# One quarter of a weight load split at partition 119

## The reference, cut to what matters

```python
for e in range(N_EXPERTS):
    gate = jnp.minimum(hf @ w_gate[e] + b_gate[e], SWIGLU_LIMIT)
    up = jnp.clip(hf @ w_up[e] + b_up[e], -SWIGLU_LIMIT, SWIGLU_LIMIT)
    act = gate * jax.nn.sigmoid(SWIGLU_ALPHA * gate) * (up + 1.0)
    y = y + combine[:, e:e + 1] * (act @ w_down[e] + b_down[e])
```

## Time and profile before

| | us |
|---|---|
| median of 3 runs | 1167.24 (1167.2 to 1167.29) |
| the profiled execution, its own time | 1170.19 |
| its span in the trace | 1168.4 |
| PE busy | 1123.5 (96%) |
| DVE busy | 361.7 (31%) |
| ACT busy | 256.8 (22%) |

### The profile page before, as it was taken

One profiled execution on the slowest core, in us unless ns is written; L12 is line 12 of the kernel. 1 busy time (PEld: TensorE's weight loads), 2 busy tenths in 40 slices (PEclk: granted clock), 3 DMA queues, 4 the chain that ended last, 5 costly groups with the idle time before them and its releaser, 6 DMA issues.

```text
span 1168.4 us, 14913 instructions
## 1 busy us (share of the span) xinstructions
PE 1123.5 (96%) x6081; PEld 560.4 (48%) x6081; DVE 361.7 (31%) x877; ACT 256.8 (22%) x528; POOL 15.6 (1%) x20
## 2 busy tenths in 40 slices
PE   8999999999999999999999989998989998999988
PEld 8998989874343434243433333333333433443333
DVE  5566765641213222212121212121212121222213
ACT  6566554431101101111111110111010111110102
POOL 1000000000000000000000000000000000000000
PEclk9999999989999999999999989999999998999999
DMA  9865546789999999999999999999999999999995
GB/s 301 293 179 182 163 153 223 300 358 416 426 429 426 428 435 431 430 431 431 431 430 432 431 432 431 430 430 430 430 430 434 430 431 429 430 426 430 427 424 216
DMA packets 52782, 445.52 MB, mean 381 GB/s; under 512 B 3715, under 2 KB 32057, under 8 KB 37489
## 3 DMA queue, kind: packets, MB, share of 16 engines
q1 hardware_dynamic: 50666, 439.83, 90.5%
q0 software_dynamic: 1248, 4.20, 1.3%
q10 hardware_dynamic: 806, 0.59, 0.2%
HBM read 443.47 MB, written 1.13 MB: 381 GB/s over the span
## 4 chain that ended last, share of the span: by engine, by line
PE 68%; DMA 27%; ACT 1%; issue 1%; DVE 1%; ACTq 0%; SPq 0%; DVEq 0%
PE psum L1312 25%; DMA ring<-in_w_up 25%; PE psum L1337 13%; PE psum L1235 5%; PE psum L953 4%; PE psum L955 4%; PE psum L954 4%; PE psum L1250 4%; DMA ring<-in_w_down 2%; PE psum L1258 2%; PE psum L1044 1%; PE psum L998 1%; PE psum L1080 1%; PE psum L1056 1%; ACT pieces L708 1%
## 5 line engine op out<-in xcount | busy, mean ns | idle before, releaser
L1312 PE MATMUL psum<-ring,xT 128*64 128x512 f32 x960 | 435.1, 610 | 36.0 <-DMA ring<-in_w_up 35.1
L1313 PE MATMUL psum<-ring,xT 128*64 128x512 f32 x960 | 435.3, 610 | 0.0
L1312 PEld LDWEIGHTS psum<-ring,xT 128*64 128x64 f32 x960 | 132.1, 140 | 313.3 <-issue 298.6
L1337 PE MATMUL psum<-ring,guT 128*64 128x512 f32 x992 | 226.5, 598 | 1.4 <-DMA ring<-in_w_down 0.7
L1750 DVE COPY gu<-psum 128x512 f32<-128x512 f32 x32 | 33.5, 1047 | 574.2 <-PE psum L1313 574.2
L1313 PEld LDWEIGHTS psum<-ring,xT 128*64 128x64 f32 x960 | 132.1, 140 | 0.0
L1337 PEld LDWEIGHTS psum<-ring,guT 128*64 128x64 f32 x992 | 65.9, 136 | 137.2 <-issue 113.6
L893 ACT COPY gu<-psum 128x512 f32<-128x512 f32 x32 | 33.9, 1061 | 416.8 <-PE psum L1313 416.8
L1468 DVE TENSOR_TENSOR pieces<-raw,pieces 128x2048 fp32r<-128x2048 f32 x31 | 71.2, 2301 | 33.1 <-ACT pieces L708 33.0
L953 PE MATMUL psum<-hT_hi,pieces 128*128 128x256 f32 x272 | 78.4, 288 | 0.0
L954 PE MATMUL psum<-hT_lo,pieces 128*128 128x256 f32 x272 | 76.9, 283 | 0.0
(11 more groups left out here) (194 smaller groups left out, 1011.0 us busy)
## 6 DMA issues: line engine op xcount, KB each, us to landing
ring<-in_w_down SPq DMA_DIRECT2D x25, 4096.0 KB, 20.8
ring<-in_w_up SPq DMA_DIRECT2D x24, 4096.0 KB, 29.0
ring<-in_w_gate SPq DMA_DIRECT2D x23, 4096.0 KB, 30.1
ring<-in_w_gate SPq DMA_DIRECT2D x15, 2048.0 KB, 18.1
ring<-in_w_up SPq DMA_DIRECT2D x15, 2048.0 KB, 15.7
raw<-in_w_in SPq DMA_DIRECT2D x22, 1024.0 KB, 5.5
ring<-in_w_down SPq DMA_DIRECT2D x11, 2048.0 KB, 13.4
raw<-in_w_branch_a SPq DMA_DIRECT2D x4, 1024.0 KB, 5.1
```

The costliest lines, as they stand in the source:

```text
L1312: mm(every(bank(GU + nb)[0:CAP, :]), x_k, of_chunks(gate[:, k, :], nb), start=k == 0, stop=k == KC - 1)
L1313: done = mm(every(bank(GU + nb)[CAP:P, :]), x_k, of_chunks(up[:, k, :], nb), start=k == 0, stop=k == KC - 1)
L1337: done = mm(o[half * CAP:(half + 1) * CAP, :], values[:, k, :], down[:, k, half * BANK:(half + 1) * BANK], start=k == 0, stop=k == KC - 1)
```

## The change

The gate matrix of expert 22 no longer comes as one load of 4 MB but as three: its first six chunks (24 KB per partition, 128 partitions, 3 MB), then the last two chunks (8 KB per partition) for partitions 0 to 118 (952 KB), then the same chunks for partitions 119 to 127 (72 KB). All three add 16 to `place_in[1]`, and `in_place` counts three for this matrix. The wait ahead of them, and everything else, is as before.

```diff
+UNEVEN, FEWER = 3 * (E - 10), 119
...
-            return sum(SPLITS[k] if k < len(SPLITS) else not by_parts(k) for k in range(m % RING, m + 1, RING))
+            return sum(SPLITS[k] if k < len(SPLITS) else 3 if k == UNEVEN else not by_parts(k)
+                       for k in range(m % RING, m + 1, RING))
...
+            def load_uneven(m):
+                load(m, 0, KC - 2, place_in[m % RING])
+                e, kind = MATRICES[m]
+                for r in (slice(0, FEWER), slice(FEWER, P)):
+                    sp.dma_start(ring[m % RING][r, KC - 2:, :].rearrange("p c n -> p (c n)"),
+                                 weights_of[kind][e][r, KC - 2:, :].rearrange("p c n -> p (c n)")
+                                 ).then_inc(place_in[m % RING], 16)
...
                 for m in range(3 * RING, TAIL):
-                    if not by_parts(m):
+                    if m == UNEVEN:
+                        free(m, 1)
+                        load_uneven(m)
+                    elif not by_parts(m):
                         free(m, 1)
                         load(m, 0, KC, place_in[m % RING])
```

## The result

| | before | after |
|---|---|---|
| median of the runs | 1167.26 us (4 runs) | 1181.18 us (1180.34 to 1181.42, 4 runs) |
| ratio of the two | | 1.0113, 95% interval 1.0101 to 1.0125 (from the runs of one chip) |
| the profiled execution, its own time | 1170.19 us | 1180.34 us |
| its span | 1168.4 us | 1178.5 us |

The change costs 13.9 us by the medians (the ratio in the table is worked out on its own; the two medians give 1.0119). I had forecast 3.1 us, in a range that ended at 1175.5.

What follows compares the result with a forecast made beforehand. The full DMA stream was taken to bound the kernel. 3.05 us for more bytes plus 5 us of excess, less 5 us covered by a lead, gave +3.1 us: 1170.3 us, range 1165.3 to 1175.5.

Steps and rivals of the forecast that it cites:

- What bounds the kernel: Whole kernel: the DMA stream is full at about 430 GB/s, so loads that land later move the end later.
- Two more issues on SP: SP's queue at the changed matrix: two more DMA issues take 0.9 us, hidden by SP's waits.
- The cut in equal shares: The two narrow loads: 119 partitions go as 17 on each of 7 engines, 9 as one on each of 9.
- The excess: Around the uneven loads: engines in each other's way, 30 engine-us scaled from down_bias, 5 us on the worst writing engine.
- The cover by a lead of 5 us: End of the stream: the seven engines run ahead of the late ones, which hides 5 us of their 8.05 us delay.
- rival (c): The seven engines include late ones and get in each other's way: +5.2 to +8.1 us, 1174 taken; chance 0.21.
- the longer wait at expert 23: PE before expert 23's products: a longer wait was to show if the forecast was right.
- a few per cent under 430: GB/s at full share for 5 to 10 us, about 20 to 30 us after the uneven loads' issue.
- the wait at 1115 us: PE's wait for the up matrix of expert 23: near 6 us was expected for 2.89 before.
- the tail of half the engines: Stream's end: before, about eight engines finish late; forecast a tail of few, share 0.2 to 0.4 for some us.
- the 3.05 us: Uneven load: an engine of the seven carries 80 KB more and so ends 3.05 us later.
- Rival (a): The late engines carry less and nobody is in the way: end 1.9 us earlier, at most 2.4, 1165.3; chance 0.17.

Runs made afterwards that it cites:

- experts 12 and 7: The change made at the gate of expert 12, or of expert 7, in place of 22: 1178.80 against 1168.01 us, and 1177.87 against 1167.60 us.
- 119/9 alone: Changed kernel, with SP draining all earlier loads before the two uneven ones and waiting for these before the next: 1185.22 against 1167.67 us, ratio 1.0142.
- 127: Changed kernel with its two narrow loads cut at 127 and 1 partitions: 1218.2 against 1167.89 us before the change, ratio 1.0423.
- 119/9: The change itself, last two chunks cut into 119 and 9 partitions, against the kernel before: 1181.18 against 1167.26 us, ratio 1.0113.
- 115: Changed kernel with its two narrow loads cut at 115 and 13 partitions: 1176.36 against 1167.60 us before the change, ratio 1.0076.
- 114: Changed kernel with its two narrow loads cut at 114 and 14 partitions: 1179.92 against 1167.60 us before the change, ratio 1.0103.
- 123/5: Changed kernel with its two narrow loads cut at 123 and 5 partitions: 1182.75 against 1167.67 us before the change, ratio 1.0120.
- 64/64: Changed kernel with its two narrow loads cut at 64 and 64 partitions: 1174.71 against 1167.89 us before the change, ratio 1.0058.
- 120/8: Changed kernel with its two narrow loads cut at 120 and 8 partitions: 1174.74 against 1167.89 us before the change, ratio 1.0050.
- 125/3: Changed kernel with its two narrow loads cut at 125 and 3 partitions: 1175.58 against 1167.67 us before the change, ratio 1.0066.
- the whole matrix by 64 partitions: Expert 22's whole 4 MB gate matrix in two loads of 64 partitions, against the kernel before: 1182.08 against 1168.01 us, ratio 1.0123.
- the quarter in one load: Changed kernel with the last two chunks (1 MB) as one load of all 128 partitions: 1168.67 against 1167.89 us before the change, ratio 1.0004.

## Why the prediction was wrong

**What bounds the kernel** stood, and so did the sign: slower. The stream is full, and what it loses comes back nowhere: 9.2 us of the 13.9, lost in one stretch of 25 us, and 8.5 and 7.3 us at experts 12 and 7.

**Two more issues on SP** cost nothing, as forecast: 0.70 us, with SP waiting behind. It held only for seven engines; with one engine they take 24.59 us.

**The cut in equal shares** stood: 0.44 of the engines for 119/9 alone, 0.06 for 127. The Trainium skill's rule in "DMA: Bandwidth & Descriptors", section "Why a DMA increments its semaphore by 16 and not by 1", agrees with both.

**The excess was the step that failed, by its size.** I scaled by bytes: 30 engine-us. Measured are 9.2 us x 16 = 147. The down_bias load is small and comes as the stream runs out, so few others were there to be held up; that this made its row too small is argued, not shown. The cost is not one of the load's own bytes. It is a rate for the whole stream (225 in place of 430 GB/s) times the time in which several writers are at it, and that time holds the writers' rows at 0.6 us each plus the spread of the engines. Bytes of others pay most. For 119/9 the slow time is 19 us: 17 x 0.6 = 10 us are the rows, and 9 us are left for the spread. An estimate for these 9: a laggard's 4 us of work, as they show in the drained stream, take 8 us at half rate. Half of 19 us is 9.5, for 9.2 measured, but the 9 was read from this same stretch, so only its agreement with the drained stream is a check.

**The cover by a lead of 5 us was the second.** I let the seven be leaders at a little over one half. The runs at 115 and 114 speak for a laggard in sixth place, and for leads in the first five. A lead covers the bytes that an engine carries more; it cannot cover a loss of the whole stream, and the spread stretched the slow time. By its conditions this is nearest to rival (c), at +5.2 to +8.1, which took the same 30 engine-us. Its upper end was the end of my range, which is why the range missed. A slip beside it: the chances of the cases add up to 0.29 for no change and 0.62 for slower, where I had written 0.31 and 0.60.

**What I looked for in the profile:** the longer wait at expert 23 came at expert 22 already, as 12.1 us; "a few per cent under 430" was one half; the wait at 1115 us did not grow, since PE had lost more by then than the loads. The time to landing of the uneven loads is in no view. At the end of the stream the tail of half the engines is gone, as I had looked for, and one or two engines are left, where I had 0.2 to 0.4:

```profile
1160.00:1162.00 2.00, 2.00 (x12) 0.72 (x10) 0.00 (x0) 1.77 (x3) 0.00 (x0) 1.00 0.45 184
1162.00:1164.00 2.00, 2.00 (x10) 0.59 (x8) 0.00 (x0) 0.40 (x2) 0.00 (x0) 1.00 0.11 45
```

So the count of bytes behind the 3.05 us, mostly carried by leaders, has the rows on its side; it is not what the time is lost by. Rival (a), the relief of the laggards, was never seen: no cut gained anything. Whether moving 64 KB off the laggards would gain 2 us if nobody were in the way is open, as no load was found that does the one without the other.

What stays open: over all cuts, the time against before less what the windows of the slow stretch show is 4.7 us for 119/9, 4.2 for 123/5, 3.4 for 114/14, 1.5 for 115/13, but 0.3 to 0.6 for 64/64, 120/8 and 125/3, and -0.3 for the whole matrix by 64 partitions. A part of it has a place. From 885 to 1140 us the stream moves 424, 424 and 423 GB/s with 119/9, 123/5 and 114/14, and 428 or 429 with the five others and with the quarter in one load: 2.4 to 3.0 us of the stream are lost there by the three alone. It is the second dip again. In these three PE's one long wait (12.1, 17.4 and 13.4 us) is longer by 2.9 to 6.5 us than what the stream lost (9.2, 10.9 and 8.9), so PE becomes later than its loads and frees places too late; the whole matrix has a wait of 12.2 us, but for 14.4 us lost in the stream, and no dip, and 115/13 has 7.7 us for 7.3. This fits the eight kernels and was not tested by a run of its own. About 2 us are left for 119/9 and 123/5 by the medians (by the traces of 119/9, 0.1), and 2.3 and 3.0 us at experts 12 and 7, where there is no second dip.

Three more things stay open: why three writers are enough to halve the stream, whether the loss arises where the partitions are written or where the rows are read, and what makes half of the engines late. The instruction fetches have about the right size (56 engine-us), but no run separated them.

## What to carry to other kernels

When a kernel is bound by its stream of loads, keep every load in it 128 partitions wide: a narrower or oddly cut one does not cost its own bytes, in this kernel it slowed all the loads that ran beside it for as long as its last engine took. Read the DMA share together with GB/s: a full share at half the rate means that the engines hold each other up, a share that falls means that engines have nothing to do because a load was issued late. A small price read from the edge of a stream is no price for its middle; multiply by the time and by the number of engines that it holds up, not by the bytes.

## What the runs showed of the hardware that I had not expected

A full-width stream of 16 engines at 430 GB/s falls to about 225 GB/s while a load that is cut over three, five or seven engines runs in it, and to about 373 with one that lies on a single engine. Two loads of 64 partitions in place of one of 128 cost 6.8 us for 1 MB. A load whose rows all go to one engine holds up its own issue (24.59 us for two) and the next (16.46 us), so that 15 engines stood idle at a share of 0.06. And the engines of a stream that is never dry drift apart: at 852 us about half of them are some 4 us behind, at the end 5 to 7, which by the runs at experts 7 and 22 lengthens such a disturbance (15 us and 19).
